# Token attention of a two-block transformer kernel: score banks, key pieces and the place of the modulation products

## The reference

```python
for l in range(DEPTH):                      # DEPTH = 2
    mod_x = (silu_c @ w_ada[l] + b_ada[l])[:, None, :]      # 6 x 1024 values
    ...
    hx = modulate(rms_norm(x, g_norm1[l]), sh1_x, sc1_x)    # 512 image tokens
    hc = modulate(rms_norm(ctx, g_norm1[l]), sh1_c, sc1_c)  # 256 context tokens
    ...
    oa, oa_t = mixer_a(...)   # 8 query heads of 64 on 2 key heads, over 512 + 256 keys
    ob, ob_t = mixer_b(...)   # 4 heads of 64; a windowed position bias on the 512 image keys
    oc, oc_t = mixer_c(...)   # differential: softmax(q1 k1) - lambda softmax(q2 k2), 4 heads, then a norm per head
    x = x + gt1_x * (jnp.concatenate([oa, ob, oc], axis=-1) @ w_out[l])
    hx2 = modulate(rms_norm(x, g_norm2[l]), sh2_x, sc2_x)
    x = x + gt2_x * conv_ffn(hx2, ...)
```

## Time and profile before

| | us |
|---|---|
| median of 3 runs | 3678.22 (3675.38 to 3680.5) |
| span of the profiled execution | 3674.5 |
| PE busy | 3542.3 |
| DVE busy | 1740.4 |
| ACT busy | 1525.6 |
| POOL busy | 1458.9 |

### The profile page before, as it was taken

The page is one execution under the profiler, slowest core; times in us unless marked ns, Lnnn a source line. Parts: engine busy times, 40 slices in busy tenths (PEclk is TensorE's granted clock), DMA queues, the critical chain, the costliest instruction groups (busy, mean ns, idle before and its releaser), DMA issues.

```text
span 3674.5 us, 50083 instructions
## 1 busy us (share of the span) xinstructions
PE 3542.3 (96%) x19796; PEld 2813.1 (77%) x19796; DVE 1740.4 (47%) x2922; ACT 1525.6 (42%) x2558; POOL 1458.9 (40%) x986
## 2 busy tenths in 40 slices
PE   7999898999999999899999989999999989999998
PEld 5776566888899776578887768878887768888886
DVE  5766634433344766633542686161114676162114
ACT  4445544433355446534332355443223345443222
POOL 4520023544488520035444435344444434434442
PEclk8999998999999999999999999999999999999999
DMA  7613512333365421523333213223333212313331
GB/s 229 159 48 116 172 47 69 98 98 96 94 183 173 122 54 36 161 84 97 98 95 98 75 35 100 85 71 97 97 96 79 75 41 81 103 58 102 94 98 58
DMA packets 642466, 355.59 MB, mean 97 GB/s; under 512 B 70469, under 2 KB 614841, under 8 KB 642233
## 3 DMA queue, kind: packets, MB, share of 16 engines
q1 hardware_dynamic: 630379, 339.66, 32.0%
q10 hardware_dynamic: 11854, 12.72, 1.2%
HBM read 346.28 MB, written 6.05 MB: 96 GB/s over the span
## 4 chain that ended last, share of the span: by engine, by line
PE 89%; DVE 5%; ACT 3%; issue 2%; DMA 1%; POOL 1%; SPq 0%; ACTq 0%; DVEq 0%
PE psum L850 68%; PE psum L1055 5%; PE psum L1088 3%; PE psum L1106 2%; PE psum L874 1%; DVE neg_max L1920 1%; ACT work L1507 1%; PE psum L1135 1%; PE psum L954 1%; PE psum L878 1%; PE psum L1010 1%; PE psum L905 1%; PE psum L897 1%; DMA w_ada_first<-in_w_ada_dram 1%; PE psum L1113 1%
## 5 line engine op out<-in xcount | busy, mean ns | idle before, releaser
L833 POOL TENSOR_TENSOR w_lo<-w_raw,w_hi 128x256 fp32r<-128x256 f32 (+3 forms) x936 | 1397.0, 1512 | 2140.3 <-ACT w_hi L1358 2139.9
L850 PE MATMUL psum<-h_hi,w_hi 128*128 128x512 f32 (+1 forms) x2864 | 1078.7, 377 | 2.5 <-POOL w_lo L833 1.5
L850 PE MATMUL psum<-h_lo,w_hi 128*128 128x512 f32 (+1 forms) x2864 | 1054.5, 368 | 0.0
L850 PE MATMUL psum<-h_hi,w_lo 128*128 128x512 f32 (+1 forms) x2864 | 1054.1, 368 | 0.0
L1358 ACT ACTIVATE w_hi<-w_raw 128x1024 fp32r<-128x1024 f32 (+1 forms) x546 | 570.9, 1047 | 651.3 <-PE psum L850 618.2
L850 PEld LDWEIGHTS psum<-h_hi,w_hi 128*128 128x128 f32 x2864 | 541.5, 189 | 115.4 <-issue 20.2
L850 PEld LDWEIGHTS psum<-h_lo,w_hi 128*128 128x128 f32 x2864 | 541.5, 189 | 97.3 <-issue 9.9
L850 PEld LDWEIGHTS psum<-h_hi,w_lo 128*128 128x128 f32 x2864 | 541.3, 189 | 89.7
L850 PE MATMUL psum<-hid_hi,w_hi 128*128 128x512 f32 (+1 forms) x1040 | 393.0, 378 | 2.2 <-POOL w_lo L833 1.6
L850 PE MATMUL psum<-hid_lo,w_hi 128*128 128x512 f32 (+1 forms) x1040 | 391.9, 377 | 0.0
L850 PE MATMUL psum<-hid_hi,w_lo 128*128 128x512 f32 (+1 forms) x1040 | 391.9, 377 | 0.0
(11 more groups left out here) (225 smaller groups left out, 4055.8 us busy)
## 6 DMA issues: line engine op xcount, KB each, us to landing
w_raw<-in_w_up_dram SPq DMA_DIRECT2D x132, 512.0 KB, 3.8
w_raw<-in_w_ff_dram SPq DMA_DIRECT2D x128, 512.0 KB, 3.9
w_raw<-in_w_in_dram SPq DMA_DIRECT2D x92, 512.0 KB, 3.9
w_raw<-in_w_ada_dram SPq DMA_DIRECT2D x80, 512.0 KB, 4.2
w_raw<-in_w_down_dram SPq DMA_DIRECT2D x48, 512.0 KB, 3.6
w_raw<-in_w_mkv_dram SPq DMA_DIRECT2D x32, 512.0 KB, 3.8
w_raw<-in_w_down_dram SPq DMA_DIRECT2D x24, 384.0 KB, 3.1
w_ada_first<-in_w_ada_dram SPq DMA_DIRECT2D x4, 2048.0 KB, 17.9
```

The source lines that it names most:

```text
L833: m = nc.gpsimd.tensor_tensor(WL[:, c % NSPLIT, k:k + step, :], RAW[:, c % NRAW, k:k + step, :], WH[:, c % NSPLIT, k:k + step, :].bitcast( ...
L850: m = pe.matmul(out_ap, lhs(a, k), rhs(b, k), start=(k == 0 and n == 0), stop=(k == nk - 1 and n == 2))
```

## The change

1. The window steps come last: steps 0 to 15 plain, 16 to 31 differential, 32 to 39 window.
2. A lane has three score banks instead of two, 1536 columns, in which steps of even and odd number have 768 each. Of these 512 (the "long" piece) fill a bank of their own and 256 (the "short" piece) half of the bank between. PE writes the long piece of step i + 1 at the end of its iteration i, and the short piece at the start of iteration i + 1, when the exponentials of step i are done.
3. Plain and window steps are transposed back into the bank of their own long piece, the rest into bank 7; ACT, DVE and (in window steps) ACT once more copy them. Differential steps are transposed one by one, in two fills of bank 7, both copied by ACT (the second fill waits for the first one's copy), between the two short pieces.
4. The output of a turn has one block of 128 columns in bank 6. Its reciprocals are spread, copied and used for each turn, not for each group.
5. The modulation pieces are four tiles by 256 columns, two pieces a block; in steps 8 to 31 (layer 0) and 16 to 31 (layer 1), so that a block is copied and turned in every such step.
6. The window mask is added to the bias tables by POOL; the bias of step i + 1 is added by DVE at the end of its iteration i. The norm of the differential groups moves from behind the last step into steps 33 to 41; its Sqrt stands in step 37 between two exponentials, with an ACT_TABLE_LOAD ahead of it and another ahead of the next exponential.
7. The context attention keeps its old form.

The diff, cut to its core:

```diff
-            add(("ada", l, b, j), "w_ada", l, 2 * j, 2, [(0, 4 * P, 4 * P * b)])
+            add(("ada", l, b, j), "w_ada", l, 4 * j, 4, [(0, 2 * P, 2 * P * b)])
...
-ADA_LAST = 36
+ADA_END = 32
 
 
 def ada_beside(key, step):
 
-
-    if key[0] != "att" or key[1] != "x":
+    if key[0] != "att" or step < 0:
         return []
-    l = key[2]
-    parts = [(l, b, j) for b in range(ADA_FIRST, 12) for j in range(4)]
-    if l == 0:
-        parts += [(1, b, j) for b in range(ADA_FIRST) for j in range(4)]
-    pair = step - ADA_LAST + len(parts) // 2
-    return parts[2 * pair:2 * pair + 2] if pair >= 0 else []
+    if key[1] == "c":
+        return []
+    parts = [(key[2], b, j) for b in range(2 * ADA_FIRST, 24) for j in range(2)]
+    if key[2] == 0:
+        parts += [(1, b, j) for b in range(2 * ADA_FIRST) for j in range(2)]
+    first = ADA_END - len(parts) // 2
+    return parts[2 * (step - first):2 * (step - first) + 2] if step >= first else []
...
+        def attention_plan_x(layer):
+
+            steps, turns, groups = [], [], []
...
+            for m in range(4):
+                plain(m, 4, values(0))
+                groups.append(dict(tile=m, diff=False, last=len(steps) - 1, turn=len(turns) - 1))
+            for j in range(2):
+                for t in range(4):
+                    i = len(steps)
+                    for e in range(2):
+                        steps.append(dict(diff=True, lanes=[lane(64 * e + 32 * m, 32, 9 + j, 11 + j, t) for m in range(2)],
+                                          bias=None, half=e))
+                    turn([(i, 0), (i + 1, 0)], values(384 + 128 * j), t)
+                groups.append(dict(tile=6 + j, diff=True, last=len(steps) - 1, turn=len(turns) - 1))
+            for j in range(2):
+                plain(5 + j, 7 + j, values(P + 128 * j), [window(2 * j + m) for m in range(2)])
+                groups.append(dict(tile=4 + j, diff=False, last=len(steps) - 1, turn=len(turns) - 1))
+
+            S = ("att", "x", layer)
...
+                turned_at.setdefault(i + (2 if st["diff"] else 1), []).append(i)
+            for q, u in enumerate(turns):
+                u["pv_at"] = u["after"] + (3 if steps[u["after"]]["diff"] else 2)
+                pv_at.setdefault(u["pv_at"], []).append(q)
+            ada_at, side = {}, {}
+            for i in range(n):
+                for block in ada_last(S, i):
+                    ada_at[i + 1] = block
+            for o in diffs:
+                groups[o]["sum_at"] = max(groups[o]["last"] + 5, ADA_END + 1)
+                side[groups[o]["sum_at"]] = ("sum", o)
+            std_at = groups[diffs[-1]]["last"] + 6
+            for m, o in enumerate(diffs):
+                for half in range(2):
+                    side[std_at + 1 + 2 * m + half] = ("spread", (o, half))
+                groups[o]["hi_at"] = std_at + 3 + 2 * m
+            for o, g in enumerate(groups):
+                if not g["diff"]:
+                    g["hi_at"] = g["last"] + 3
+            return dict(S=S, layer=layer, steps=steps, turns=turns, groups=groups, turned_at=turned_at, pv_at=pv_at, side=side,
+                        ada_at=ada_at, std_at=std_at, diffs=diffs, length=max(g["hi_at"] for g in groups) + 2)
+
+        def region(i, m):
+
+            lane = PS[:, 3 * m:3 * m + 3, :].rearrange("p b c -> p (b c)")
+            return lane[:, i % 2 * NK:i % 2 * NK + NK]
+
+        def probs(i, m):
...
+                        pool.wait_ge(*at("tab_in", ("win", l)))
+                        for h in range(B_HEADS):
+                            nc.gpsimd.tensor_tensor(TB[:, h], TB[:, h], WINDOW.unsqueeze(1).broadcast_to([P, 14, 64]),
+                                                    ALU.add).then_inc(*mark("win_bias", (l, h)))
...
+                def score_long(i):
+                    if i == 0:
+                        for signal in before:
+                            pe.wait_ge(*signal)
+                    elif i == 1:
+                        pe.wait_ge(*before_second)
+                    elif steps[i - 2]["diff"]:
+                        pe.wait_ge(*at("exp_done", (S, i - 2, 1)))
+                    else:
+                        pe.wait_ge(*at("pt_copied_act", (S, i - 2)))
+                        pe.wait_ge(*at("pt_copied_dve", (S, i - 2)))
+                    for m, (q, k) in enumerate(steps[i]["lanes"]):
+                        ins = pe.matmul(region(i, m)[:, keys_long(i)], q, k[:, 0:SEQ], start=True, stop=True)
+                    ins.then_inc(*mark("long_done", (S, i)))
+
+                def score_short(i, lanes):
+                    if i:
+                        pe.wait_ge(*at("exp_done", (S, i - 1, lanes[-1])))
+                    for m in lanes:
+                        q, k = steps[i]["lanes"][m]
+                        pe.matmul(region(i, m)[:, keys_short(i)], q, k[:, SEQ:NK], start=True, stop=True).then_inc(
+                            *mark("scores_done", (S, i, m)))
+
+                def turn_ada(i):
+                    block = att["ada_at"][i]
+                    pe.wait_ge(*at("ada_rows", block))
+                    pe.wait_ge(*at("exp_done", (S, i - 1, 0)))
+                    ada_turn(AROW, 2, lambda n: spare(i)[:, 2 * n:2 * n + 2]).then_inc(*mark("ada_turned", block))
...
+                def out_free(i):
+
+                    done = sum(u["pv_at"] < i for u in turns)
+                    if done:
+                        pe.wait_ge(*at("o_step", (S, done - 1)))
+                    if i - 1 in att["side"]:
+                        pe.wait_ge(*at("side_taken", (S, i - 1)))
+                    if ada_rows:
+                        pe.wait_ge(*at("ada_rows", ada_rows[-1]))
+
+                def value(q):
+                    u = turns[q]
+                    i = u["after"]
+                    if steps[i]["diff"]:
+                        pe.wait_ge(*at("pt_copied_act", (S, i, 1)))
+                    else:
+                        pe.wait_ge(*at("pt_copied_act", (S, i)))
+                        pe.wait_ge(*at("pt_copied_dve", (S, i)))
+                        pe.wait_ge(*at("rest_copied_act" if steps[i]["bias"] else "rest_copied_dve", (S, i)))
+                    if q:
+                        pe.wait_ge(*at("o_step", (S, q - 1)))
...
+                score_long(0)
+                for i in range(att["length"]):
+                    turned = att["turned_at"].get(i, ())
+                    plain = [j for j in turned if not steps[j]["diff"]]
+                    mixed = [j for j in turned if steps[j]["diff"]]
+                    if i in att["ada_at"]:
+                        turn_ada(i)
+                    if i < len(steps):
+                        score_short(i, (0,) if mixed else (0, 1))
+                    for j in mixed:
+                        turn_mixed(j, 0)
+                    if mixed and i < len(steps):
+                        score_short(i, (1,))
+                    for j in mixed:
+                        turn_mixed(j, 1)
+                    for j in plain:
+                        turn_plain(j)
+                    out_free(i)
+                    if i in att["side"]:
+                        side(i)
+                    for q in att["pv_at"].get(i, ()):
+                        value(q)
+                    ada(S, i, ada_rows, X_SIDE)
+                    if i + 1 < len(steps):
+                        score_long(i + 1)
...
+                def recips(i):
+                    for block in ada_last(S, i):
+                        act.wait_ge(*at("w_used", IDS["ada", block[0], block[1], 1][0]))
+                        if ada_rows:
+                            act.wait_ge(*at("ada_turned", ada_rows[-1]))
+                        nc.scalar.activation(AROW[:, :], X_SIDE, ACT.Copy).then_inc(*mark("ada_rows", block))
+                        ada_rows.append(block)
+                    for q in att["pv_at"].get(i, ()):
+                        act.wait_ge(*at("pv_done", (S, q)))
+                        if q >= 2:
+                            act.wait_ge(*at("o_step", (S, q - 2)))
+                        nc.scalar.activation(recip_rows(q), X_RECIP, ACT.Copy).then_inc(*mark("recip_copied", (S, q)))
...
+                    if i == att["std_at"]:
+                        act.wait_ge(*at("side_taken", (S, i - 1)))
+                        nc.scalar.activation(SUBS[:, :, :], SUBS[:, :, :], ACT.Sqrt, bias=EPSC[:, 0:1],
+                                             scale=1.0 / HEAD).then_inc(*mark("sub_std", S))
...
+                n = len(steps)
+                for i in range(att["length"]):
+                    if 0 < i <= n and not steps[i - 1]["diff"]:
+                        copy_plain(i - 1)
+                    if i < n:
+                        exp(i, 0)
+                    if 2 <= i < n + 2 and steps[i - 2]["diff"]:
+                        copy_mixed(i - 2, 1)
+                    if 0 < i <= n and steps[i - 1]["bias"]:
+                        copy_rest(i - 1)
```

(43 more changed lines are left out.)

325 lines of the change are left out of this document (253 added, 72 removed).

## The result

The changed kernel takes 3724.14 us (median of 4 runs, 3711.06 to 3727.63), the kernel before 3679.31 on the same chip: ratio 1.0118, 95% interval 1.0105 to 1.0131. It is slower, as forecast, but by 44.8 us and not by 19.6, and its median lies above the range's end of 3714. The profiled execution is the one of 3727.63 us, with a span of 3725.8, 51.3 more than before. The four executions differ as their mean granted clocks do: the one of 3711.06 has 0.974, the one of 3727.63 has 0.968.

What follows compares the result with a forecast made beforehand. PE, 96% busy, and an equally long loop through the other engines bound a plain step at 4.60 us. Layers +10.4 and +4.4, less 3.2, plus 8 gave +19.6: span 3694, median 3697.8 us; range 3671 to 3714.

Steps and rivals of the forecast that it cites:

- tail: From the last step's first exponential to the output projection: 10.3 us against 13.54 and 13.35 before.
- Plain steps: Steps 0 to 15: PE's work sets 4.71 us a step, 6.25 with products; the first two save 1.7 once.
- Differential steps: Steps 16 to 31: PE sets steps with values, a loop through ACT and DVE those without; 92.9 us a layer.
- 8 x 6.20 + 8 x 5.41 = 92.9: Differential steps of a layer: eight with values at 6.20 us, eight without at 5.41 us.
- The loop through ACT and DVE: Differential steps without values: row copy queued behind the second exponential, then turn, short piece, maximum, exponentials; 5.41 us.
- Rival C: PE idling at seam and Sqrt lowers the clock: 13 us per layer at most, half hidden; 3711 us, chance 0.18.
- Rivals A and B: A: PE sets differential steps, 4.97 us, total 3671, chance 0.17. B: window-step bias hidden, 4.71 us, total 3680, chance 0.15.
- Window steps: Steps 32 to 39: a 5.98 us loop through DVE's scaling and adds, plus seam, square and Sqrt; 52.6 us together.
- the seam chain: Steps 33 and 34: second value product waits for the first's scaling, long piece and bias behind; 2.6 + 3.1 us extra.
- the root's two loads: Step 37: Sqrt between two Exps needs two table loads of 1.28 us each; 2.9 us net with the Sqrt.
- The allowances: Whole sum: 8 us added for half-clock stretches and hand-overs, 3.2 us taken off for the output projection's clock.
- The 3.2 in the output projection: First output projection products ran at the lower clock before; 1.6 us per layer counted as gained.

Runs made afterwards that it cites:

- The filler experiments: Five unused 128-column multiplications added per differential step without products to the changed kernel with products in plain steps: 3710.68 us on 128 rows, 3755.22 on 32.
- the version with the value in step 33: Changed kernel with the last differential turn's value product moved from step 34 to step 33: 3707.87 us, ratio 1.0079.

## Why the prediction was wrong

By its steps, forecast first:

| | forecast | layer 0 | layer 1 |
|---|---|---|---|
| plain, without products | 36.0; 73.7 | 36.15 | 73.31 |
| plain, with products | 50.0 | 50.92 | none |
| differential | 92.9 | 109.64 | 109.04 |
| window, to step 39 | 52.6 | 54.78 | 54.77 |
| tail | 10.3 | 10.07 | 10.08 |

- *Plain steps:* right, the sums partly by luck. A step is 4.63 against 4.71, with products 6.34 against 6.25, and the first steps save 0.8 to 0.9 and not 1.7, which makes up for the first difference.
- *Differential steps:* this step failed. It is the term "8 x 6.20 + 8 x 5.41 = 92.9", which measured 109.6 and 109.0, 32.8 more in both layers together. The term took full clock for granted. 41.0 and 37.5 us went by at half clock, and since PE has next to no room with the products in these steps, nearly half of that is lost (17.6 and 17.0 against 92.0, the 8 x 11.5 of the steps at full clock). The work itself was priced well in the sum, by luck: the steps with values take 6.6 against 6.20, those without 5.0 against 5.41. The loop through ACT and DVE is the one named, but two exponentials with the copy between them fill 2.0 us where 2.5 was put, and a lone short piece takes some 0.6 (from its start to the next weight load) where 0.43 was put. The filler experiments show the cause of the half clock as far as they go: with full-array work in every step it is all but gone, with the same amount of lean work it grows.
- *Rival C* had the mechanism and not the place: it looked for the clock's fall at the idle of the seam and of the root, from the earlier trace rows, and priced 13 us a layer, half of it hidden. At the seam it came as well (3.2 us in step 33), but most of it came where PE hardly waits. I read the half clock as following idle time; no part of the argument asked what kind of work stood in a stretch.
- *Rivals A and B* did not happen. At full clock the steps take 5.0 and 6.6, not A's 4.11 and 5.82, and the window steps 5.7, not B's 4.71. A was nearer than it looks: PE's own work fills a step without values to within some 0.1 us, since its pieces are longer than A had them.
- *Window steps:* the seam chain and the root's two loads came as worked out, 8.0 + 10.0 where the clock held in step 33, against 8.6 + 9.1, and 8.4 + 7.7 at the root against 8.9 + 7.6. The loop is 5.7, not 5.98. That DVE's order sets the loop is not borne out by the edit that turned it round.
- *The allowances*, 8 for half clock and hand-overs less 3.2 in the output projection, were the place where the clock stood in the sum: 4.8 in all, where 17.6 + 17.0 in the differential steps and 3.2 x 2 in step 33 was due. The 3.2 in the output projection is not borne out: all that follows the attention is 1.0 us shorter.
- *Slips in the sums:* the terms of the tail add up to 10.2 and not 10.3, those of the window steps to 52.7 and not 52.6; they cancel.

Put together: 37.5 us beyond the sums per layer (+10.4 and +4.4) up to the output projections (32.9 differential, 4.4 window, 0.7 plain, -0.5 tail), less the allowance of 4.8, less 1.0 after them, is the 31.7 by which the span's growth of 51.3 exceeds 19.6.

**What stays open.** Why the same differential work has a clock of 0.96 and 0.92 in the kernel before and of 0.81 and 0.83 here. It isn't the products' presence, TensorE's waits, or the lone short pieces, each tried. The length of the steps, that is, how thin the full-array work lies in time, is not excluded: the kernel before with the long piece twice has steps of 5.46 and 6.01, 11.5 a pair as here, and a clock of 0.93 and 0.86, the latter what the changed kernel has at its best (0.87). The order of the pieces within a step was not tried apart. Nor is it shown which lean work counts: the filler tells 32 rows from 128, while products on few output columns were not told apart.

Even at full clock the change would hardly win, by an estimate from these runs. The profiled execution of the version with the value in step 33 took 3701.0, with stages of 106.5 and 104.3; with 92.0 in both it would take 3674, against 3679 of the kernel before, 0.1% less, and the kernel before has half clock of its own, 20 us in steps 24 to 38. What the plain steps gain (4.63 against 4.82 with their group ends) goes into the seam, the root and products that no longer have the window steps to stand in.

## What to carry to other kernels

A sum of instruction lengths holds at one clock level; for each stage ask which share of TensorE's instructions uses few rows, and price the stage at half clock as well when a change packs such work together. To tell idle from lean work as the cause of a low clock, add the same filler twice, once on the whole array and once on a part. Where two pipelines of different depth meet, look for the step in which both deliver: moving one product by a step gave back 8 to 10 us (16 in one comparison, in which the clock helped), while filling for the clock gave back nothing, because the filler stood on the bound engine.

## What the runs showed of the hardware

- TensorE at 99% busy ran at a granted clock of 0.73 when the added work used 32 rows, and at 1.00 when the same number of instructions used 128 (layer 1's differential steps).
- A full busy share is no sign of full clock: 108.2 of 109.6 us busy, clock 0.81.
- The time at half clock in a stage varied between profiled executions of the same differential instructions by 20 us (27.3 to 47.8).
- Between two instructions of ACT, a switch of function tables cost 1.30 us each way, with no drain.
